# A fused two-block kernel: first FFN steps, modulation sums and value products laid out anew

## The reference, cut to what matters

```python
x = x + 0.5 * swiglu(rms_norm(x, ffn1_norm), ffn1_w_gate, ffn1_w_up, ffn1_w_down)
f = einsum('gts,bcsge->bctge', tril(w_s), v_chunks) + b_s       # gMLP, 8 groups of 64 features
mod = (silu(c) @ w_mod + b_mod)                                 # 1024 x 6144, one row
sh1, sc1, g1, sh2, sc2, g2 = split(mod, 6)
probs = softmax_with_sink(q k' / 8 + bias, window 128)          # 8 query heads, 2 key heads
y_attn = einsum("bnhgqk,bnkhd->bnqhgd", probs, v_band)          # head size 64
```

## Time and profile before

| | us |
|---|---|
| median of 3 runs (1824.13 to 1830.53) | 1825.98 |
| the profiled execution's own time | 1825.67 |
| its span | 1824.1 |
| PE busy | 1785.1 (98%) |
| DVE busy | 1056.7 (58%) |
| ACT busy | 727.6 (40%) |
| POOL busy | 183.7 (10%) |
| products of line 1919, sum of the three kinds | 1153.7 |

### The profile page before, as it was taken

One profiled execution on the slowest core, in us unless ns is written; L12 is line 12 of the kernel. 1 busy time (PEld: TensorE's weight loads), 2 busy tenths in 40 slices (PEclk: granted clock), 3 DMA queues, 4 the chain that ended last, 5 costly groups with the idle time before them and its releaser, 6 DMA issues. The chain is left out here.

```text
span 1824.1 us, 23599 instructions
## 1 busy us (share of the span) xinstructions
PE 1785.1 (98%) x8872; PEld 1454.4 (80%) x8872; DVE 1056.7 (58%) x1479; ACT 727.6 (40%) x1011; POOL 183.7 (10%) x239
## 2 busy tenths in 40 slices
PE   8999999999999999999899999999998999999998
PEld 6788888878888677888788888887985778888887
DVE  5766536564563666554788753445585556655433
ACT  3222222233443887523233222224556345555322
POOL 4222001120000000005210120120000400000000
PEclk9999999999999999999899999999999999999999
DMA  7766422333222212223555552335022223322222
GB/s 212 235 218 218 145 85 79 103 122 114 95 70 92 70 47 70 70 93 104 169 171 149 157 168 67 104 98 192 28 113 70 70 92 104 103 92 80 92 90 84
DMA packets 171692, 206.79 MB, mean 113 GB/s; under 512 B 18404, under 2 KB 150114, under 8 KB 171106
## 3 DMA queue, kind: packets, MB, share of 16 engines
q1 hardware_dynamic: 144994, 161.97, 27.6%
q0 software_dynamic: 12640, 38.55, 6.8%
q10 hardware_dynamic: 13984, 5.27, 1.2%
HBM read 190.29 MB, written 17.56 MB: 114 GB/s over the span
## 5 line engine op out<-in xcount | busy, mean ns | idle before, releaser
L660 ACT CAST w_hi<-w_raw 128x2048 fp32r<-128x2048 f32 x158 | 301.3, 1908 | 741.7 <-PE bank L1919 382.9
L1145 DVE TENSOR_TENSOR w_lo<-w_raw,w_hi 128x2048 fp32r<-128x2048 f32 x158 | 367.2, 2324 | 377.0 <-ACT w_hi L660 376.5
L1919 PE MATMUL bank<-h_hi,w_hi 128*128 128x512 f32 x1056 | 414.9, 393 | 6.6 <-DVE w_lo L1145 5.3
L1919 PE MATMUL bank<-h_hi,w_lo 128*128 128x512 f32 x1056 | 412.5, 391 | 0.0
L1919 PE MATMUL bank<-h_lo,w_hi 128*128 128x512 f32 x1056 | 326.3, 390 | 1.6 <-DVE h_lo L1183 1.6
L1919 PEld LDWEIGHTS bank<-h_hi,w_hi 128*128 128x128 f32 x1056 | 199.2, 189 | 51.3 <-issue 5.0
L1919 PEld LDWEIGHTS bank<-h_lo,w_hi 128*128 128x128 f32 x1056 | 198.8, 188 | 43.7 <-DVE h_lo L1183 2.0
L1919 PEld LDWEIGHTS bank<-h_hi,w_lo 128*128 128x128 f32 x1056 | 199.2, 189 | 41.0
L1876 PE MATMUL bank<-hid_hi,w_lo 128*128 128x512 f32 x528 | 205.4, 389 | 0.0
L1876 PE MATMUL bank<-hid_hi,w_hi 128*128 128x512 f32 x528 | 205.4, 389 | 0.0
L1876 PE MATMUL bank<-hid_lo,w_hi 128*128 128x512 f32 x528 | 205.4, 389 | 0.0
(11 more groups left out here) (432 smaller groups left out, 2498.7 us busy)
## 6 DMA issues: line engine op xcount, KB each, us to landing
w_raw<-in_w_in SPq DMA_DIRECT2D x29, 1024.0 KB, 5.1
mod_raw<-in_w_mod POOLq DMA_DIRECT2D x96, 256.0 KB, 3.7
w_raw<-in_ffn_w_gate SPq DMA_DIRECT2D x22, 1024.0 KB, 5.4
w_raw<-in_ffn_w_up SPq DMA_DIRECT2D x22, 1024.0 KB, 5.4
w_raw<-in_w_up SPq DMA_DIRECT2D x22, 1024.0 KB, 5.0
w_raw<-in_ffn_w_down SPq DMA_DIRECT2D x16, 768.0 KB, 4.7
w_raw<-in_ffn_w_down SPq DMA_DIRECT2D x16, 640.0 KB, 4.0
w_raw<-in_w_out SPq DMA_DIRECT2D x8, 1024.0 KB, 5.2
```

The source lines that it names most:

```text
L660: act.copy(w_hi[i % 2][:], w_raw[i % 2][:]).then_inc(S("w_hi_done"), 1)
L1145: dve.tensor_tensor(w_lo[s][:], w_raw[s][:], w_hi[s][:].bitcast(F32), ALU.subtract).then_inc(S("w_split"), 1)
L1919: mm = pe.matmul(bank[:], w[:, k, at], h[:, k, :], start=k == first and part == 0 and i == 0, stop=k == last and part == 1)
```

## The change

1. `PHASES` of the first FFN: step 7 becomes a loop of its own, so that its last product can close the accumulation.
2. POOL asks for the first four pieces of the first group ahead of the clearing (first FFN) and ahead of the S5 loads (second FFN); the other four pieces follow behind these.
3. DVE copies all eight x tiles and only the low part of tile 0 between them; low parts 1 to 7 come after. `first_gate` goes through all eight tiles with the high parts and then with the low parts.
4. The modulation's sum over partitions is turned round: the stationary operand is `row_of`, 128 x 8 with ones in the column of the group's number, and the moving operands are the high and low part, 128 x 512. All groups of an FFN accumulate into eight rows of bank 6. After the 11 steps DVE's copy of the rows is turned by four transposes into bank 5. DVE makes `row_of` anew for each group and copies the rows once for each FFN.
5. gMLP: the loop over chunks is outside, that over halves inside.
6. Window attention: values are kept once; each product is made in two halves of 64 output partitions, each with its own two heads (256 columns) moving; ACT needs one copy for the values of a block and one to take a unit's output.

```diff
-PHASES = {"ffn1": ((0, 1, True, None), (1, BESIDE_STEPS, True, None), (BESIDE_STEPS, GU_STEPS, False, None)),
+PHASES = {"ffn1": ((0, 1, True, None), (1, BESIDE_STEPS - 1, True, None), (BESIDE_STEPS - 1, BESIDE_STEPS, True, None), (BESIDE_STEPS, GU_STEPS, False, None)),
...
+            def group(i, first, ks):
+
+                for k in ks:
+                    pool.wait_ge(S("mod_step"), i * MOD_STEPS + (first * MOD_STEPS + k + 1))
+                    pool.dma_start(mod_raw[:, k % MOD_SLOTS, :], wm[:, k, bass.ds(i * T + first * T, T)])\
+                        .then_inc(S(f"mod_landed{k % MOD_SLOTS}"), 16)
+
+            def beside(name, between, behind=None):
...
+                group(0, first, range(MOD_SLOTS))
+                between()
+                group(0, first, range(MOD_SLOTS, KD))
+                if behind:
+                    behind(0)
+                with pool.Fori(1, groups) as i:
+                    group(i, first, range(KD))
...
-                for twice in range(2):
-                    act.copy(v2[:, b, :, twice, :], B[b][:, NKV * QK:2 * NKV * QK].rearrange("p (n d) -> p n d", n=NKV)).then_inc(S("kv2_out"), 1)
+                act.copy(v2[:, b], B[b][:, NKV * QK:2 * NKV * QK].rearrange("p (n d) -> p n d", n=NKV)).then_inc(S("kv2_out"), 1)
...
-                o = B[7][:].rearrange("p (j two q) -> p j two q", j=2, two=2)
-                for half in range(2):
-                    rows_of = slice(64 * half, 64 * half + 64)
-                    act.copy(yat[rows_of, 2 * n:2 * n + 2, b * P:(b + 1) * P], o[rows_of, :, half, :]).then_inc(S("sw_out"), 1)
+                act.copy(yat[:, 2 * n:2 * n + 2, b * P:(b + 1) * P], B[7][:, 0:2 * P].rearrange("p (j q) -> p j q", j=2)).then_inc(S("sw_out"), 1)
...
                 dve.wait_ge(S("mod_acc_free"), g + 1)
+                dve.tensor_copy(row_of[:], one_hot[:, bass.ds(row * -1 + 7, 8)])
...
+                        dve.tensor_copy(tmp[0:8, 4, :], B[6][0:8, :]).then_inc(S("rows_made"), 1)
...
-            for k in range(KD + 3):
-                if k < KD:
-                    dve.wait_ge(S("x_t"), k + 2)
-                    dve.tensor_copy(x[:, k, :], B[2 + k % 4][:]).then_inc(S("x_turned"), 1)
-                if k >= 3:
-                    scaled_lo("n1", lambda k: gain1[:, k:k + 1], (k - 3, ))
+            for k in range(KD):
+                dve.wait_ge(S("x_t"), k + 2)
+                dve.tensor_copy(x[:, k, :], B[2 + k % 4][:]).then_inc(S("x_turned"), 1)
+                if k == 3:
+                    scaled_lo("n1", lambda k: gain1[:, k:k + 1], (0, ))
+            scaled_lo("n1", lambda k: gain1[:, k:k + 1], range(1, KD))
...
-                for k in range(KD):
-                    for wait, h in ((ready_hi, h_hi), (ready, h_lo)):
+                for wait, h in ((ready_hi, h_hi), (ready, h_lo)):
+                    for k in range(KD):
...
-                            for s4 in range(4):
-                                for part in (mod_hi, mod_lo):
-                                    mm = pe.matmul(B[6][:, bass.ds(i * 8 + 2 * s4, 2)], part[:, s4 * P:(s4 + 1) * P], ones_r[:],
-                                                   start=part is mod_hi, stop=part is mod_lo)
+                            for part in (mod_hi, mod_lo):
+                                mm = pe.matmul(B[6][0:8, :], row_of[:], part[:],
+                                               start=start == 0 and part is mod_hi, stop=stop == MOD_STOP[name] and part is mod_lo)
...
+                    if name in PHASES and stop == GU_STEPS:
+                        pe.wait_ge(S("rows_made"), list(PHASES).index(name) + 2)
+                        for s4 in range(4):
+                            mm = pe.transpose(B[5][:, 8 * s4:8 * s4 + 8], tmp[0:8, 4, s4 * P:(s4 + 1) * P], ident[0:8, 0:8])
+                        mm.then_inc(S("rows_t"), 1)
...
-                for half in range(2):
-                    g = 2 * f + half
-                    for c in range(TB):
+                for c in range(TB):
+                    for half in range(2):
+                        g = 2 * f + half
...
-                products(B[7][:], [(v2[:, b - 1 + kb, n].rearrange("p w d -> p (w d)"), pT[:, u % 2, kb, :]) for kb in SW_BLOCKS[u]])\
-                    .then_inc(S("sw_pv"), 1)
+                for kb in SW_BLOCKS[u]:
+                    heads = pT[:, u % 2, kb, :].rearrange("p (j two q) -> p two j q", j=2, two=2)
+                    for half in range(2):
+                        mm = pe.matmul(B[7][64 * half:64 * half + 64, 0:2 * P].rearrange("p (j q) -> p j q", j=2), v2[:, b - 1 + kb, n, :],
+                                       heads[:, half], start=kb == SW_BLOCKS[u][0], stop=kb == SW_BLOCKS[u][-1])
+                mm.then_inc(S("sw_pv"), 1)
```

More of the change, by code:

```diff
@@ L184, in build @@
         log_dt = sb("log_dt", [P, 2 * NS])
-        ones_r = sb("ones_r", [P, 2], F32R)
+        one_hot = sb("one_hot", [P, 16])
+        row_of = sb("row_of", [P, 8], F32R)
+        sb("up_to_a_line", [P, 16])
         def col(name, i):
@@ L611, in _, with s5_loads @@
             wait_x(pool, "mixer", KD - 1)
[L613 to L624 removed]
+            def s5_loads():
+                for i, part in enumerate(("re", "im")):
+                    for half in range(2):
+                        for k in range(4):
+                            s5_b = inp[f"ssm_b_{part}_2"].rearrange("o (k t j) n h -> k t n (o j) h", k=4, t=2)[k, half]
+                            pool.dma_start(b_in[64 * half:64 * half + 64, i, 4 * k:4 * k + 4], s5_b).then_inc(S("s5_landed"), 16)
+                    c_v = inp[f"ssm_c_{part}_2"].rearrange("o (c g) h n -> (g h) (o c) n", c=4)
+                    for twice in range(2):
+                        pool.dma_start(c_in[:, i, :, twice, :], c_v).then_inc(S("s5_landed"), 16)
+                done(pool.iota(rot_ti[:, 0:NPOW], pattern=[[1, NPOW]], base=0, channel_multiplier=0))
+                done(pool.iota(rot_ti[:, NPOW:], pattern=[[CHUNK, NC]], base=0, channel_multiplier=0))
+                pool.tensor_copy(rot_t, rot_ti[:]).then_inc(S("rot_t_made"), 1)
+            beside("ffn2", s5_loads)
             for p in range(NS // 2):
@@ L1329, in swiglu @@
                         if mods:
-                            modulation(i + MOD_AT[name])
+                            modulation(i + MOD_AT[name], i)
                         if start == 0 and name == "ffn2":
@@ L1356, in swiglu @@
                 last_col = 4 * groups
-                dve.tensor_tensor(mod[:, first:last_col], B[6][:, 0:2 * (last_col - first):2], cols("b_mod_2")[:, first:last_col],
-                                  ALU.add).then_inc(S("mod_made"), 1)
+                dve.wait_ge(S("rows_t"), list(PHASES).index(name) + 5)
+                turned = B[5][:, 0:32].rearrange("p (s g) -> p g s", s=4)[:, 0:groups - MOD_AT[name], :]
+                dve.tensor_tensor(mod[:, first:last_col].rearrange("p (g s) -> p g s", s=4), turned,
+                                  cols("b_mod_2")[:, first:last_col].rearrange("p (g s) -> p g s", s=4), ALU.add).then_inc(S("mod_made"), 1)
             def down(name, factor, beside=()):
```

39 lines of the change are left out of this document (16 added, 23 removed).

## The result

The kernel after takes 1846.8 us (median of 4 runs, 1842.04 to 1849.17), the one before 1825.88 beside it: a ratio of 1.0107, interval 1.0091 to 1.0122. It is slower by 21 us, where I forecast 11 us less and gave "slower" 0.03. The profiled execution is the quickest of the four: 1842.04, span 1840.3.

The account below looks back on a forecast made before the run. PE, busy 1785.1 of 1824.1 us, was taken as the bound. Terms −2.3 − 2.8 − 1.4 + 1.5 − 0.8 − 5.2 = −11.0 took 1825.67 to 1814.7 us; range 1809.5 to 1821.

Parts of the forecast that it names:

- halves that do not overlap: Rival, window-attention values and gMLP: halves run singly and each change of half is paid; +9.1, 1834.8 us, chance 0.04.
- start up to `first_gate`: x tiles and first gate panel: reordered copies and high parts first move nothing on PE; cost 0.
- FFN1, end of step 0 to step 1: First FFN's start: earlier piece requests let DVE's group and PE's step 1 begin earlier; −2.3 us, bounds 0 and −5.3.
- modulation sums, dense groups: Sums over partitions in nine dense groups: 0.90 us falls to 0.75 each; −1.4 us.
- turning of the rows, twice: Four new transposes ending each FFN's gate and up, on PE's path: 0.75 us each time; +1.5, bounds +0.9 and +3.
- gMLP: gMLP products with halves in turn: 64 passes in 3.7 us, was 4.54; −0.8 us, bounds 0 and −1.1.
- FFN2, end of step 0 to step 1: Second FFN's start: first four pieces requested before S5 loads, PE's step 1 earlier; −2.8 us, bounds 0 and −4.8.
- clock and stands behind these starts: PE behind the first FFN's start: same clock fall expected after a single stand of nearly 3 us; no term.
- value products: Window attention: 56 half passes, two at once, replace 28; −5.2 us, bounds −2.6 and −6.5, 0 if not at once.
- the clock stays up: Rival: one shorter stand in each FFN's start keeps PE at 2.4 GHz, 1.5 us more each; 1811.7 us, chance 0.10.
- the DMA wait in front of DVE's fifth piece: Sign in the new trace that would show the prediction wrong; no size given.
- 8 columns cost no change: Bound of the modulation sums: no tile-size cost, 0.55 us a group, gain 3.2 us in all.

Follow-up runs that it names:

- good layout: Kernel after with one_hot and row_of behind all other tiles, so h_hi is at its old byte; 1813.3 us, ratio 0.9916.
- S5 first: Kernel after, h_hi at its old byte, with the second FFN's S5 loads ahead of its first modulation requests again; 1817.56 us, ratio 0.9944.
- both sides 128 bytes on: Kernel after, h_hi at its old byte, then weight panels and h, hid all moved 128 bytes further; 1812.41 us.
- first filled version: Kernel after, h_hi at its old byte, plus unread products: twelve in first FFN's step 0, eight in second FFN's step 3; 1811.26 us, ratio 0.9914.
- whole values: Kernel after, h_hi at its old byte, window-attention value products whole again (28 passes, values copied twice); 1815.41 us, ratio 0.9946.

## Why the prediction was wrong

The step that failed is the measure at its head: "0.227 us for 512 columns in the one-pass kind", used for products that the change does not touch, as if they were the same after it. They went to 0.2327, 37 us in sum. I had priced every instruction that the diff adds or moves and never asked where its three new tiles push the others. The price is on no row of the trace before, which knows one layout only, but the move itself could be read from the declarations that the change adds. No rival had it either: the one that ended on the slower side, halves that do not overlap, did not come true.

With the layout put back, the sum can be held against the traces of before and of the good layout, whose spans are 12.0 us apart (forecast 11.0; median 1813.3 against 1814.7). That the totals agree so well is in part luck: the start (1.9, not forecast) and the modulation sums (2.2 more) are outweighed by clock and stands (2.9) and the values (1.0). Each entry is a difference between the two traces' starts of the same products:

| term | forecast | measured |
|---|---|---|
| start up to `first_gate` | 0 | −1.9 |
| FFN1, end of step 0 to step 1 | −2.3 | −2.1 |
| modulation sums, dense groups | −1.4 | −3.6 (8 x 0.45) |
| turning of the rows, twice | +1.5 | +1.2 |
| gMLP | −0.8 | −0.8 |
| FFN2, end of step 0 to step 1 | −2.8 | −3.4 |
| clock and stands behind these starts | 0 | +2.9 |
| value products | −5.2 | −4.2 |
| rest | | −0.1 |

- *First FFN, step 0: right.* DVE's group begins 0.12 us behind the root's end in the new trace, PE's step 1 is late by the panel's low part (line 1159), as forecast. In the trace of after the start is at 43.80, earlier than the 46.8 I gave, because the whole start came 2.5 us earlier and the pieces faster. The clock stayed at full speed there and fell in the good layout: between my forecast and its rival "the clock stays up" it varies from execution to execution, and the forecast was right in 11 of 14 traces. One sign of being wrong that I named was no sign: the DMA wait in front of DVE's fifth piece is there (1.44 us at 35.56), but it was there in the trace before, too:

```profile
39.96 0.75 DVE L1306 SCALAR_TENSOR_TENSOR mod_acc<-mod_raw,small,mod_acc 128x512 f32<-128x512 f32 x1 [1.14 <-DMA mod_raw<-in_w_mod]
```

- *Second FFN, step 0: right* (−3.4, bounds 0 and −4.8). With S5 first again the trace loses 2.4 by step 4.
- *Missed: what DVE gives back two steps later.* In step 2 DVE's work is dense (the S5 angles, then the group), so it hands over the panel's low part only 9.9 us earlier than before where PE comes 10.6 earlier. PE's idle time grows from 1.00 to 2.00 us, and in this trace the clock falls behind it, 1.6 us (in four of seven such traces, above). It does so with S5 first too, so the loads' place is not the cause.
- *Modulation sums: mis-sized.* I charged 0.10 for the change to 8 columns each way and 0.1 for a bare load. Nothing of it shows: from the first sum to the next product is 0.47 in the new trace (111.84 to 112.31), two products' pace and no more. The gain is 0.45 a group, beyond even my bound "8 columns cost no change", which still held 0.1 for the load: 3.6 us from the eight groups that were dense, where the bound gave 3.2 for nine. The Trainium skill, TensorEngine Tiling (Array Packing), section Key Properties, says that changing the tiling mode drains the engine; between 128 and 8 output columns this trace shows no such price, and between 128 and 64 some 0.1 us each way remains (516.77 to 517.10).
- *Turning of the rows: about right.* 0.34 us for the four and some 0.1 each side.
- *gMLP: right*, 4.47 to 3.64 us, which is 0.057 us a pass; the rival of halves that run one by one is out.
- *Value products: right in kind, 1.0 too large.* The halves run two at once (eight in 1.08). The wait before unit 7 stayed (2.89 us for 2.71); it is released by ACT's copy of the unit before.
- *x copies: 0 forecast, 1.9 earlier in the traces;* undoing the edit gives back 0.9 us at `first_gate` in the trace and 0.2 at step 1, where DVE's group decides. I put the other 1.0 down to the landing of x; `first_gate` began between 15.2 and 16.2 us in the seven traces with a good distance and this edit. In the times no gain of this edit is clear of the scatter.
- *Range:* its lower end does not come out of its own working: 1811.7 less the 1.3 between −5.2 and −6.5 is 1810.4, not 1809.5. Nothing hangs on it.

In the profiled execution of after, the 37 us are partly hidden: its span is 28.2 us over that of the good layout, since two clock falls fewer give 3.3, and the start gives 0.6. Slow products ahead of a stand of PE cost nothing, which I take to be the other 5.0; no run shows it by itself.

## What to carry to other kernels

Before counting instructions, list which tiles a diff moves: a table of a few bytes, declared ahead of the large tiles, can reprice every product of 512 columns. For one-pass products of 512 columns like these, try a distance of a multiple of 256 bytes between stationary and streamed tiles, put small tables behind the large ones, and when a kernel is off, divide a window's length by its count of products before looking at any wait. If a wait of PE goes, look one or two steps on for the engine that now comes last, and at the granted clock behind the stand that it makes.

## What the runs showed of the hardware

- One-pass products of 512 columns (fp32, high and low parts) run at 226.8 ns when stationary and streamed operand lie a multiple of 256 bytes apart, and at mean paces of 229.8 to 233.4 ns at distances of 32, 64, 128 and 192 bytes beside it: up to 2.9%. It is their distance and neither's own place, and it has a direction: streamed less stationary 64 bytes over a multiple of 256 gave 229.1 and 230.0 ns, 192 bytes over it 233.3 and 233.8.
- Other shapes did not slow down. One-pass products of 256 columns took 119.9 ns at the good distance, 118.7 in the kernel after and 113.4 with `h` 64 bytes on. Two-pass products took 109 ns for 128 columns (turnings by `ident`) and 429 ns for 512 (the sums of `yat_sq` and `ys_sq` with `ones`), before and in the traces with these tiles 32, 64, 128 and 192 bytes further apart.
- The Trainium skill, TensorE: Matmul & The Clock Gate, section Step-by-step: what each phase is for, says that weights and streamed operand have read ports of their own and that loading the next weights takes no SBUF bandwidth from the running product. The pace here depends on the distance between the tiles that these two reads fetch (226.8 to 233.4 ns), so at 512 columns the two reads do not look independent in this kernel; how they meet no run here shows.
- Behind a stand of 2.1 to 4.8 us between two starts PE's granted clock was 0.50 for about 3 us (1.6 us lost) in some executions and not in others: ahead of the second FFN's step 3 a stand of about 2.2 us was followed by the fall with both sides 128 bytes on, and not in the first filled version, and ahead of the first FFN's step 1 a stand of 3.24 us was followed by it in the good layout, and not with whole values.
